# First expert's weights fetched and half split during the routing, first chunk peeled, rotary tables moved to the last chunk, in a two-layer mixture-of-experts trunk

## Chip, cores and metric

One core of one Trainium2 chip. The metric is the device time of one execution in microseconds (us), the median of several executions of the same program.

## What is computed

A two-layer trunk over 4096 tokens of width 1024, all in float32 outside. Layer 0 is a causal pooling mixer, layer 1 a sliding-window attention with rotary queries and keys; each is followed by the same hierarchical mixture of experts and a gated per-layer embedding. The change touches the mixture of experts and the place of the rotary tables:

```python
expert_id = gsel * EXPERTS_PER_GROUP + eidx         # 32 experts, 2 for each token
order = jnp.argsort(flat_e)                         # tokens sorted by expert
xs = xt[stok]
a = jax.nn.silu(lax.ragged_dot(xs, w_gate, sizes)) * lax.ragged_dot(xs, w_up, sizes)
y = lax.ragged_dot(a, w_down, sizes) * sg[:, None]
out = jnp.zeros((T, D), y.dtype).at[stok].add(y)
cos, sin = rope_tables(positions)                   # used only in and after layer 0's combining
```

Each expert has three float32 matrices (gate and up 1024x512, down 512x1024), 6 MB in all.

## The kernel before

The kernel is written as phases; each is a block with one program for each engine, and a block begins when all engines have ended the one before. In order: constants, pooling mixer, then `route_phase`, `experts_phase`, `combine_phase` for layer 0, the attention, `route_phase`, `experts_phase` for layer 1, and the final combining.

**Routing.** VectorE (DVE) works alone through a chain of some 150 small operations: group and expert of each token, a rank of each token in its expert, a table of chunks, and at last eight blocks of one-hot matrices that TensorE (PE) turns into the list of tokens. In layer 0 alone the block carries other work beside it: the embedding product `up`, 32 tiles of 24 bf16 matmuls. ScalarE (ACT) copies each half tile from PSUM to one of three buffers `up_out` (`take_up`, L568), and SyncE (SP) stores each tile (L550). PE has two PSUM banks for it, so it may be two half tiles ahead of ACT; ACT takes tile t only when the store of tile t-3 has landed. SP's program in this block is: two loads of `wu_raw`, four 1 MB loads of `pT`, then the 32 stores.

**Experts.** The sorted tokens are cut into chunks of up to three tiles of 128 rows of one expert; here there are 32 chunks in each layer, numbered q, with weights in buffer u = q mod 2. The products run in a split of float32 into two bf16 parts: for each weight chunk c of six (0, 1 gate; 2, 3 up; 4, 5 down), SP loads 1 MB into `raw[c]` (L832), ACT makes the high part `w_hi` (L883), and POOL (c = 0 to 2) or DVE (c = 3 to 5) makes the low part `w_lo` (L825). `raw` is single: the load of the next expert's c waits for the low part. The token rows are gathered by three indirect DMAs of POOL (L916) and turned by three DMA transposes of SP (L838) into the single `xT`. PE then makes gate and up for four blocks f of 128 columns, with two PSUM banks each; ACT does the silu (L894), DVE three operations for each f (`gated`, L951 to L955), and PE the down product, 24 matmuls for each tile; DVE copies it to `y` (L967), SP stores it (L857).

Steady order on SP for chunk q: loads of expert q+2, then the transposes of q+1 once gate and up of q are done, then the stores of q. On ACT for chunk q: high parts 4, 5 of q+1, four silus, high parts 0 to 3 of q+2.

**Opening of the phase.** SP loads expert 0 (in layer 0 after the rotary positions), waits for all three gathers, turns, loads expert 1 as the low parts free `raw`, and in layer 0 waits for the rotary sines and stores the tables. ACT makes six high parts, in layer 0 the two sines, then four high parts of expert 1, and only then enters the chunks and its first silu. In layer 0 DVE starts with the 11 chained rotary operations (L1124 to L1137).

## Time and profile before

| | |
|---|---|
| median of 3 runs | 5163.12 us (5152.84 to 5165.77) |
| the profiled execution | 5158.74 us |
| its span | 5157.1 us |
| PE busy | 4617.6 us (90%) |
| DVE, ACT, POOL busy | 2868.5, 1985.6, 1582.1 us |
| mean DMA rate | 232 GB/s |

The span runs from the first instruction to the last. Times in the trace count from the span's start. The routing of layer 0 stands at about 291 to 400, its experts at 400 to 1592; the routing of layer 1 at 3385 to 3472, its experts at 3472 to 4690. A busy share of an engine is an average over the stages; what a stage is worth has to be read at the wait that ends last there.

### The profile page before, as it was taken

How to read it: one execution, taken by the hardware profiler on the slowest of the kernel's cores; microseconds unless marked ns; L12 is line 12 of the kernel's file. 1: busy time of each engine (PE TensorE's matmuls, PEld its weight loads, DVE VectorE, ACT ScalarE, POOL GpSimd, SP SyncE). 2: the span in 40 equal slices, each digit the busy share in tenths (PEclk: the TensorE clock that was granted, in tenths of full speed). 3: DMA queues.
4: the chain of work that ended last, by engine and by line, in shares of the span. 5: the costliest groups of instructions: out<-in, count | busy, mean ns of one | idle time of the engine just before them, and what ended most of it. 6: DMA issues, size and time to landing. Idle time of an engine off the chain costs nothing. (4 is left out here: it accounts for less than half of the span.)

```text
span 5157.1 us, 89595 instructions
## 1 busy us (share of the span) xinstructions
PE 4617.6 (90%) x28834; PEld 2934.8 (57%) x29253; DVE 2868.5 (56%) x5893; ACT 1985.6 (39%) x2898; POOL 1582.1 (31%) x1161
## 2 busy tenths in 40 slices
PE   7985999999995999999499999936999999996999
PEld 6953766666672444444256666625666676663444
DVE  6774444444444555555388888873444444444665
ACT  6844344343432122222155555514433434332333
POOL 1104444443440111110033343304434434331332
PEclk9997999999997999999799999968999999998999
DMA  8969999999986666665377777619999999976997
GB/s 248 324 216 301 304 318 294 296 306 299 280 269 190 172 172 172 171 171 147 97 164 180 181 179 181 165 45 313 298 308 302 293 302 289 296 240 184 219 226 154
DMA packets 1265957, 1194.89 MB, mean 232 GB/s; under 512 B 945616, under 2 KB 965072, under 8 KB 1265872
## 3 DMA queue, kind: packets, MB, share of 16 engines
q1 hardware_dynamic: 1219792, 1026.04, 69.0%
q0 software_dynamic: 46080, 167.79, 10.7%
q8 instruction: 44, 0.72, 0.1%
q14 instruction: 41, 0.34, 0.0%
HBM read 717.60 MB, written 249.56 MB: 188 GB/s over the span
## 5 line engine op out<-in xcount | busy, mean ns | idle before, releaser
L825 POOL TENSOR_TENSOR ex_w_lo<-ex_raw,ex_w_hi 128x2048 bf16<-128x2048 f32 x192 | 780.7, 4094 | 1166.5 <-ACT ex_w_hi L883 1166.5
L883 ACT ACTIVATE ex_w_hi<-ex_raw 128x2048 bf16<-128x2048 f32 x384 | 707.3, 1900 | 458.8 <-PE ex_ps_y L110 189.1
L987 PE MATMUL ex_ps_gate<-ex_xT,ex_w_hi 128*128 128x0 bf16 x2048 | 571.9, 280 | 171.7 <-DMA ex_xT<-ex_xrow 130.1
L988 PE MATMUL ex_ps_gate<-ex_xT,ex_w_hi 128*128 128x0 bf16 x2048 | 571.8, 279 | 0.0
L989 PE MATMUL ex_ps_gate<-ex_xT,ex_w_lo 128*128 128x0 bf16 x2048 | 571.6, 279 | 0.0
L987 PE MATMUL ex_ps_up<-ex_xT,ex_w_hi 128*128 128x0 bf16 x2048 | 559.4, 273 | 0.0
L988 PE MATMUL ex_ps_up<-ex_xT,ex_w_hi 128*128 128x0 bf16 x2048 | 558.9, 273 | 0.0
L989 PE MATMUL ex_ps_up<-ex_xT,ex_w_lo 128*128 128x0 bf16 x2048 | 558.8, 273 | 0.0
L951 DVE TENSOR_TENSOR ex_aT<-ex_silu,ex_ps_up 128x384 bf16<-128x384 f32 x256 | 141.7, 553 | 725.5 <-PE ex_ps_up L989 549.7
L967 DVE COPY ex_y<-ex_ps_y 128x512 f32 x324 | 224.1, 692 | 567.0 <-PE ex_ps_y L110 505.3
L109 PE MATMUL ex_ps_y<-ex_w_lo,ex_aT 128*128 128x512 bf16 x1296 | 492.2, 380 | 8.5
L110 PE MATMUL ex_ps_y<-ex_w_hi,ex_aT 128*128 128x512 bf16 x1296 | 492.2, 380 | 0.0
L894 ACT ACTIVATE ex_silu<-ex_ps_gate 128x384 f32<-128x384 f32 x256 | 125.0, 490 | 900.7 <-PE ex_ps_gate L989 900.3
L825 DVE TENSOR_TENSOR ex_w_lo<-ex_raw,ex_w_hi 128x2048 bf16<-128x2048 f32 x192 | 443.6, 2312 | 19.3 <-ACT ex_w_hi L883 19.3
L1897 POOL TENSOR_TENSOR att_pr<-att_ex,att_rden 128x512 bf16<-128x512 f32 x256 | 294.4, 1150 | 518.8 <-DVE att_rden L1990 515.2
L108 PE MATMUL ex_ps_y<-ex_w_hi,ex_aT 128*128 128x512 bf16 x1134 | 431.5, 380 | 6.7 <-DVE ex_aT L955 6.7
L1920 ACT ACTIVATE att_ex<-att_score,att_nmx 128x257 f32<-128x257 f32 x512 | 256.3, 502 | 328.1 <-DVE att_nmx L1985 327.9
L987 PEld LDWEIGHTS ex_ps_gate<-ex_xT,ex_w_hi 128*128 128x128 bf16 x2048 | 204.9, 100 | 206.1 <-issue 142.8
L2077 PE MATMUL att_ps_s<-att_kT,att_qT 128*128 128x256 f32 x1024 | 270.7, 393 | 6.5 <-DVE att_kT L2040 3.1
L1980 DVE CUSTOM_DVE_ANT_0 att_score<-att_ps_s,all_mask,att_sink 128x256 f32<-128x256 f32 x496 | 218.4, 477 | 74.5 <-PE att_ps_s L2077 73.2
L108 PE MATMUL cb_ps_b<-cb_wg,cb_xT 128*128 128x512 bf16 x511 | 195.6, 383 | 59.2 <-DMA cb_xT<-cb_x 43.1
L108 PE MATMUL cb_ps_gate<-cb_wg,cb_xT 128*128 128x512 bf16 x498 | 190.7, 383 | 41.4 <-DMA cb_xT<-cb_x 41.4
(352 smaller groups left out, 9447.0 us busy)
## 6 DMA issues: line engine op xcount, KB each, us to landing
ex_raw<-in_w_exp_gate SPq DMA_DIRECT2D x128, 1024.0 KB, 10.0
ex_raw<-in_w_exp_up SPq DMA_DIRECT2D x128, 1024.0 KB, 12.8
ex_raw<-in_w_exp_down SPq DMA_DIRECT2D x128, 1024.0 KB, 6.9
y_rows<-ex_y SPq DMA_DIRECT2D x162, 512.0 KB, 2.9
cb_hin<-h_mid SPq DMA_DIRECT2D x64, 512.0 KB, 3.7
mix_x<-in_x SPq DMA_DIRECT2D x32, 512.0 KB, 4.9
h_mid<-mix_h SPq DMA_DIRECT2D x32, 512.0 KB, 5.5
y_rows<-mix_zeros SPq DMA_DIRECT2D x32, 512.0 KB, 6.1
```

What stands on the lines that cost most here:

```text
L108: pe.matmul(out, lhs_hi, rhs_hi, start=first, stop=False)
L109: pe.matmul(out, lhs_hi, rhs_lo, start=False, stop=False)
L110: return pe.matmul(out, lhs_lo, rhs_hi, start=False, stop=last)
L825: eng.tensor_tensor(w_lo[u][:, w], raw[:, c, :], w_hi[u][:, w], ALU.subtract).then_inc(lo_done, 1)
L883: act.activation(w_hi[u][:, c * WCHUNK:(c + 1) * WCHUNK], raw[:, c, :], ACT.Copy).then_inc(hi_done, 1)
L967: dve.tensor_copy(y[:, bass.ds(j, 1), 512 * n:512 * n + 512].rearrange("p o d -> p (o d)"), ps_y[n][:]).then_inc(y_done, 1)
L987: pe.matmul(out, hi, x_hi, start=j == 0, stop=False)
L988: pe.matmul(out, hi, x_lo, start=False, stop=False)
L989: mm = pe.matmul(out, lo, x_hi, start=False, stop=j == KD - 1)
L1897: pool.tensor_tensor(pr[c % ER][:, 0, :, :], ex[c % ER][:, :, 0:W], rden[:, 2 * c:2 * c + 2].unsqueeze(2).to_broadcast([P, 2, W]), ALU.mul ...
L1920: e = act.activation(ex[c % ER][:, k, :], score[c][:, k, :], ACT.Exp, bias=nmx[:, n:n + 1], accum_out=esum[:, n:n + 1])
L2077: mm = pe.matmul(ps_s[:, c % 2, :, b * P:(b + 1) * P], qT[par][:, c, :], keys[:, jj, :, :], start=True, stop=True)
```

## The change

Three things, as one edit. First, a class `ExpertWeights` owns `raw` and the first `w_hi`, so that they live through routing and experts. `route_phase` loads expert 0 (SP, six loads, behind the `pT` loads and, in layer 0, the positions; ahead of the stores of `up`), and ACT makes its six high parts there, one after every third tile of `take_up`. Second, in `experts_phase` chunk 0 is taken out of the loop. DVE makes the low parts 0 to 3 of expert 0 and POOL 4 and 5. SP turns each gathered tile as it lands, then loads expert 1 in the order 3, 0, 4, 1, 5, 2. ACT makes the high parts of expert 1 between the silus of chunk 0; DVE makes its low part 3 after `gated` 2, and 4 and 5 after the copies of chunk 0's `y`. SP turns the rows of chunk 1 ahead of the loads of expert 2. Third, the rotary angles run on DVE in the last chunk of layer 0, in three parts after f = 0, 1, 2, in the free `raw`; ACT's sines and SP's stores come after the last chunk.

```diff
@@ route_phase
+            if rot:
+                rot.load(nc, sp, A)
+            for c in range(NCHUNK):
+                W.load(sp, c, 0).then_inc(raw_loaded[c], 16)
             for t in range(tiles):
                 sp.wait_ge(up_done, 2 * t + 2)
                 sp.dma_start(up_t[t], up_out[t % UP][:]).then_inc(up_st[t % UP], 16)
@@
-            take_up(6, NT)
+            for c in range(NCHUNK):
+                take_up(6 + 3 * c, 9 + 3 * c)
+                w_hi(c)
+            take_up(6 + 3 * NCHUNK, NT)
@@ experts_phase
+            chunk(0, 0, True, True)
             with eng.Fori(0, full) as i:
-                for u in (0, 1):
-                    chunk(2 * i + u, u, True, True)
-            chunk(2 * full, 0, True, False)
-            chunk(2 * full + 1, 1, False, False)
+                chunk(2 * i + 1, 1, True, True)
+                chunk(2 * i + 2, 0, True, True)
+            chunk(2 * full + 1, 1, True, True)
+            chunk(2 * full + 2, 0, True, False)
+            chunk(2 * full + 3, 1, False, False)
@@ SP
                 for t in range(CT):
+                    if opening:
+                        sp.wait_ge(gathered[t], 16)
                     sp.dma_start(xT[:, :, :, t * P:(t + 1) * P]..., xrow[t][:], transpose=True)
@@
-            if rot:
-                rot.load(nc, sp, A)
-            e = table(sp, 2, 0, 0, NE - 1)
-            for c in range(NCHUNK):
-                load(0, c, e)
-            sp.wait_ge(gathered, 16 * CT)
-            turn_x()
             e = table(sp, 2, 1, 0, NE - 1)
-            for c in range(NCHUNK):
+            turn_x(opening=True)
+            for c in (3, 0, 4, 1, 5, 2):
                 wait_split(sp, 0, c)
-                load(1, c, e)
-            if rot:
-                rot.store(sp)
+                load(c, e)
             full = chunks(sp, chunk)
@@
             sp.sem_inc(all_stored, 1)
+            if rot:
+                rot.store(sp)
+                sp.wait_ge(rot.stored, 32)
@@ ACT
                     act.activation(silu[f % 2][:], ps_gate[f % 2][:, 0:CW], ACT.Silu).then_inc(silu_done, 1)
+                    if opening and f > 0:
+                        for c in (2 * f - 2, 2 * f - 1):
+                            hi_part(1, 1, c)
@@
-            for c in range(NCHUNK):
-                hi_part(0, 0, c)
+            chunks(act, chunk)
             if rot:
                 rot.sines(act)
-            for c in range(4):
-                hi_part(1, 1, c)
-            chunks(act, chunk)
@@ DVE
                     gated(q, f)
-                    if follows and f < NCHUNK - POOL_CHUNKS:
+                    if follows and not opening and f < NCHUNK - POOL_CHUNKS:
                         lo_part(dve, q + 1, 1 - u, POOL_CHUNKS + f, dve_lo)
+                    if opening and f == 2:
+                        lo_part(dve, 1, 1, POOL_CHUNKS, dve_lo)
+                    if rot and not follows and f == 0:
+                        rot.angles(dve)
+                    if rot and not follows and f == 1:
+                        rot.reduced(dve)
+                    if rot and not follows and f == 2:
+                        rot.bounded(dve)
```

## Rows read from the trace of the kernel before

**Rows 1.** The page's costliest groups: busy, mean ns of one, idle before and its releaser

```profile
L825 POOL TENSOR_TENSOR ex_w_lo<-ex_raw,ex_w_hi 128x2048 bf16<-128x2048 f32 x192 | 780.7, 4094 | 1166.5 <-ACT ex_w_hi L883 1166.5
...
L825 DVE TENSOR_TENSOR ex_w_lo<-ex_raw,ex_w_hi 128x2048 bf16<-128x2048 f32 x192 | 443.6, 2312 | 19.3 <-ACT ex_w_hi L883 19.3
```

**Rows 2.** Busy time by stretch, 400 to 500 us: engines, granted clock, DMA share, GB/s

```profile
400.00:500.00 100.00, 47.80 (x360) 36.89 (x365) 51.36 (x77) 42.52 (x29) 48.00 (x21) 0.73 0.98 318
```

**Rows 3.** Waits, opening of layer 0's experts (398 to 520): total, times, longest

```profile
PE ex_ps_gate L987 <- DMA ex_xT<-ex_xrow: 39.4, 2, 36.8
...
PE ex_ps_gate L987 <- ACT ex_silu L894: 16.0, 1, 16.0
```

**Rows 4.** Waits, opening of layer 1's experts (3385 to 3560)

```profile
PE ex_ps_gate L987 <- DMA ex_xT<-ex_xrow: 33.7, 1, 33.7
```

**Rows 5.** PE's waits over layer 0's steady chunks (530 to 1580)

```profile
PE ex_ps_gate L987 <- DMA ex_xT<-ex_xrow: 27.8, 12, 4.8
```

**Rows 6.** Timeline of SP's queue in layer 0's routing: start, length, instruction

```profile
292.81 7.79 SPq L546 DMA_DIRECT2D rt_pT<-pT_rows  x4
307.03 90.61 SPq L550 DMA_DIRECT2D up_rows<-rt_up_out  x32
```

**Rows 7.** DMA issues, 290 to 400: KB each, median us from issue to landing

```profile
up_rows<-rt_up_out SPq DMA_DIRECT2D x32, 512.0 KB, 2.6
rt_pT<-pT_rows SPq DMA_DIRECT2D x4, 1024.0 KB, 11.6
```

**Rows 8.** The same view, 400 to 470

```profile
rot_sin<-ex_y SPq DMA_DIRECT2D x1, 512.0 KB, 16.9
```

**Rows 9.** Timeline of ACT in layer 0's routing: idle before and releaser in brackets

```profile
313.30 0.60 ACT L568 ACTIVATE rt_up_out<-rt_ps_up 128x512 f32<-128x512 f32 x1 [0.70 <-PE rt_ps_up L110]
...
396.68 0.60 ACT L568 ACTIVATE rt_up_out<-rt_ps_up 128x512 f32<-128x512 f32 x1 [0.70 <-PE rt_ps_up L110]
```

**Rows 10.** Timeline of SP's queue, first 85 us of layer 0's experts

```profile
402.41 2.01 SPq L832 DMA_DIRECT2D ex_raw<-in_w_exp_gate  x2
...
415.00 16.07 SPq L838 DMA_TRANSPOSE ex_xT<-ex_xrow  x3
432.58 0.95 SPq L832 DMA_DIRECT2D ex_raw<-in_w_exp_gate  x2
...
475.10 7.77 SPq L838 DMA_TRANSPOSE ex_xT<-ex_xrow  x3
```

**Rows 11.** Timeline of ACT, the same stretch

```profile
426.53 1.91 ACT L883 ACTIVATE ex_w_hi<-ex_raw 128x2048 bf16<-128x2048 f32 x1 [0.80 <-DMA ex_raw<-in_w_exp_down]
...
438.57 1.91 ACT L883 ACTIVATE ex_w_hi<-ex_raw 128x2048 bf16<-128x2048 f32 x1 [6.81 <-DMA ex_raw<-in_w_exp_gate]
...
451.59 1.91 ACT L883 ACTIVATE ex_w_hi<-ex_raw 128x2048 bf16<-128x2048 f32 x1 [0.80 <-DMA ex_raw<-in_w_exp_up]
...
469.93 0.49 ACT L894 ACTIVATE ex_silu<-ex_ps_gate 128x384 f32<-128x384 f32 x1 [4.35 <-PE ex_ps_gate L989]
...
482.91 3.71 ACT L883 ACTIVATE ex_w_hi<-ex_raw 128x2048 bf16<-128x2048 f32 x2 [3.15 <-PE ex_ps_y L110]
```

**Rows 12.** Timeline of ACT, opening of layer 1's experts

```profile
3541.44 0.49 ACT L894 ACTIVATE ex_silu<-ex_ps_gate 128x384 f32<-128x384 f32 x1 [4.97 <-PE ex_ps_gate L989]
...
3559.73 3.71 ACT L883 ACTIVATE ex_w_hi<-ex_raw 128x2048 bf16<-128x2048 f32 x2 [8.22 <-PE ex_ps_y L110]
```

**Rows 13.** Timeline of POOL: the first gather of each layer's experts

```profile
403.00 1.18 POOL L916 DMA_INDIRECT ex_xrow<-hn_rows,ex_token  x1 [0.98 <-POOL ex_token L912]
...
3474.31 1.04 POOL L916 DMA_INDIRECT ex_xrow<-hn_rows,ex_token  x1 [0.87 <-POOL ex_token L912]
```

**Rows 14.** Timeline of DVE, opening of layer 0's experts

```profile
408.17 3.74 DVE L1132 SCALAR_TENSOR_TENSOR ex_y<-ex_y 128x1024 f32<-128x1024 f32 x3
...
423.20 10.10 DVE L825 TENSOR_TENSOR ex_w_lo<-ex_raw,ex_w_hi 128x2048 bf16<-128x2048 f32 x3 [0.37 <-ACT ex_w_hi L883]
```

**Rows 15.** Timeline of DVE, last chunk of layer 0's experts

```profile
1568.15 0.56 DVE L951 TENSOR_TENSOR ex_aT<-ex_silu,ex_ps_up 128x384 bf16<-128x384 f32 x1 [2.67 <-PE ex_ps_up L989]
```

More of the change, by code:

```diff
@@ L472, in _, with __init__, load, split_hi @@
             steps(pe, step)
-def route_phase(nc, A, C, layer):
+class ExpertWeights:
+    def __init__(self, nc, A, layer, stack):
+        m = Mem(nc, f"ew{layer}", stack)
+        self.mem = m
+        self.raw = m.sb("raw", [P, NCHUNK, WCHUNK])
+        self.hi = [m.sb("hi0", [P, NCHUNK * WCHUNK], BF16)]
+        self.lo = []
+        self.layer = layer
+        halves = "l e (h k p) n -> (l e h) p k n"
+        self.src = [A[n].rearrange(halves, p=P, k=WCHUNK // w)
+                    for n, w in (("w_exp_gate", F), ("w_exp_up", F), ("w_exp_down", D))]
+    def load(self, sp, c, e):
+        part, half = divmod(c, 2)
+        return sp.dma_start(self.raw[:, c, :].rearrange("p (k n) -> p k n", k=WCHUNK // (D if part == 2 else F)),
+                            self.src[part][self.layer * 2 * NE + 2 * e + half])
+    def split_hi(self, act, u, c):
+        return act.activation(self.hi[u][:, c * WCHUNK:(c + 1) * WCHUNK], self.raw[:, c, :], ACT.Copy)
+    def split_lo(self, eng, u, c):
+        w = slice(c * WCHUNK, (c + 1) * WCHUNK)
+        return eng.tensor_tensor(self.lo[u][:, w], self.raw[:, c, :], self.hi[u][:, w], ALU.subtract)
+def moe_phase(nc, A, C, layer, rot=None):
+    with ExitStack() as stack:
+        W = ExpertWeights(nc, A, layer, stack)
+        if rot:
+            rot.open(W.mem, W.raw)
+        route_phase(nc, A, C, W, layer, rot)
+        experts_phase(nc, A, C, W, layer, rot)
+def route_phase(nc, A, C, W, layer, rot=None):
     with ExitStack() as stack:
@@ L538, in route_phase @@
             "dve_step exp_in exp_out ranked summed hot_done token_done listed chunk_mm")
+        raw_loaded = [m.sem(f"raw_loaded{c}") for c in range(NCHUNK)]
         block = stack.enter_context(nc.Block())
@@ L827, in _, with load, turn_x @@
         @block.sync
         def _(sp):
-            def load(q, c, e):
-                part, half = divmod(c, 2)
-                ap = src[part][layer * 2 * NE + 2 * e + half]
-                sp.dma_start(raw[:, c, :].rearrange("p (k n) -> p k n", k=WCHUNK // (D if part == 2 else F)),
-                             ap).then_inc(raw_loaded[c], 16)
-            def turn_x():
+            def load(c, e):
+                W.load(sp, c, e).then_inc(raw_loaded[c], 16)
+            def turn_x(opening=False):
@@ L845, in chunk @@
                         wait_split(sp, q + 1, c)
-                        load(q + 2, c, e)
+                        load(c, e)
+                opening = isinstance(q, int)
+                if refill and not opening:
+                    weights()
                 first = table(sp, 0, q, 0, MAX_TILES)
@@ L854, in chunk @@
                     turn_x()
+                if opening:
+                    weights()
                 with sp.Fori(0, tiles) as j:
@@ L879, in _ @@
             act.sem_inc(down_mm, DOWN_OPEN)
+            act.sem_inc(hi_done, NCHUNK)
             def hi_part(q, u, c):
-                act.wait_ge(raw_loaded[c], 16 * q + 16)
-                act.activation(w_hi[u][:, c * WCHUNK:(c + 1) * WCHUNK], raw[:, c, :], ACT.Copy).then_inc(hi_done, 1)
+                act.wait_ge(raw_loaded[c], 16 * q)
+                W.split_hi(act, u, c).then_inc(hi_done, 1)
             def chunk(q, u, follows, refill):
-                if follows:
+                opening = isinstance(q, int)
+                if follows and not opening:
                     first = table(act, 0, q, 0, MAX_TILES)
@@ L926, in _ @@
             gather(0)
[L927 to L928 removed]
+            for c in range(DVE_FIRST, NCHUNK):
+                W.split_lo(pool, 0, c).then_inc(pool_first_lo, 1)
             pool.wait_ge(xT_turned, 16 * CT)
@@ L968, in chunk @@
                                         ps_y[n][:]).then_inc(y_done, 1)
-            for c in range(POOL_CHUNKS, NCHUNK):
-                lo_part(dve, 0, 0, c, dve_lo)
-            if rot:
-                dve.wait_ge(rot.stored, 32)
+                if opening:
+                    for c in range(POOL_CHUNKS + 1, NCHUNK):
+                        lo_part(dve, 1, 1, c, dve_lo)
+            for c in range(DVE_FIRST):
+                W.split_lo(dve, 0, c).then_inc(dve_first_lo, 1)
             chunks(dve, chunk)
@@ L1084, in open @@
         self.inv = m.sb("inv", [P, nf])
-        self.sin, self.cos, self.turns = (room[:, i, :].rearrange("p (t f) -> p t f", f=nf) for i in range(3))
+        self.sin, self.cos, self.turns = (room[:, i, 0:NT * nf].rearrange("p (t f) -> p t f", f=nf) for i in range(3))
         self.loaded, self.step_done, self.ready, self.made, self.stored = m.sems(
```

129 lines of the change are left out of this document (70 added, 59 removed).

## Prediction

> **What bounds the kernel now.** I read the shares of busy time first, then the waits of PE in three stretches, then the queues in order of time. PE is busy for 90% of the span, so the change can only win where PE stands still for long. In the steady chunks it hardly does: 27.8 us in 1050, in 12 waits for turned rows [rows 5]. At each opening it does. In layer 0 the first product waits 36.8 us for the rows (from the last `up` tile at 396.7 to 433.5), then 16.0 us more for a silu [rows 3, 9]; in layer 1 the first of these two is 33.7 us [rows 4]. In 400 to 500 PE is busy 47.8 us at a granted clock of 0.73 while DMA is at 0.98 [rows 2]. What ends last is a queue: the gathers were issued at 403.0, but the transposes stand behind 6 MB of weights, from 415.0 to 431.1, and PE starts 2.4 us after [rows 10, 13]. The second wait is ACT's order: its high parts of expert 1 (438.6 to past 451.6) come ahead of its first silu [rows 11]. The routing of layer 1 leaves DMA and ACT nearly idle; that of layer 0 does not: PE has `up` work until 396.7, and ACT and SP serve it in step, 1.30 us for each half tile [rows 9].
>
> **Loads moved into the routing.** Layer 1: six loads and six high parts (1.91 us each) lie beside 87 us of DVE work that needs ACT twice, both times ahead of them. Cost nothing.
>
> Layer 0: the six loads are issued ahead of the `up` stores on SP's queue. Is a store held by loads ahead of it? A 512 KB store lands in 2.6 us on a free queue; the rotary store issued at 440.1, behind the loads of expert 1, took 16.9 [rows 7, 8]. So it is. The last `pT` load lands near 310.5 (issued by 300.6, median 11.6 to landing) [rows 6, 7]. Then come the positions (1.5 us, my estimate for 4-byte pieces, from 0 to the 4 us they take alone), and six loads at 2.71 us each, the step between high parts that wait for landings (0.80 idle + 1.91) [rows 11]: 328.3. The first store lands at 328.3 + 1.3 (half of a load) = 329.6, say 330. ACT takes tile 3 at 313.3 [rows 9] and needs that store. It waits 17 us, and PE, two banks ahead, stops with it, before the one-hot sums that DVE's chain needs. PE restarts at the low level of its clock: 2 us more (0 to 3). The six high parts then each stand between two takes: 0.60 + 1.91 + 0.60 = 3.11 us against the 2.6 that two banks hide, so 0.5 each, 3 at most with the semaphore's delay, partly in PE's waits for DVE: 2 (0 to 8, if none of the 1.91 is hidden). PE's work ends this block, so all of it shows. **+21 us** (from 8, if the store slips in earlier than the queue's order says, to 28).
>
> The Trainium skill, "DMA: Bandwidth & Descriptors", section on queues, rings and completion order, says that on each DMA engine descriptors are consumed in ring order and SP has one row of rings. This speaks against the change: by it the store waits for all six loads, as the row of the rotary store has it; were the queue fair to later transfers, the sum would be 17 us better.
>
> **Opening of the experts.** All times are layer 0's, counted as if its block began at 400.9 as before. Gathers are issued from 403.0; with no weights in flight the first lands some 4.3 us later (estimate: 2.6 for a 512 KB transfer [rows 7] plus POOL's 1.18 and a little), 407.3. Three transposes take 7.8 us to issue in a steady chunk [rows 10], to 415.1, and PE starts 2.4 later: 417.5, 16 us sooner. Gate and up take four times 4.84 [rows 11], plus 2 for the low clock: until 438.9.
>
> Loads of expert 1 need the turn's end, and the first needs DVE's low part 3. DVE starts at about 402.7; its four parts take 9.2 us, POOL's two 8.2 [rows 1]. Side by side they would end by 412, in turns by 420. Three parts of DVE took 10.1 us where 6.9 are due, while POOL made its own [rows 14], so I take turns, 418. By landings after a first issue at 402.4 and 432.6, the fourth load lands 19.0 us on and the sixth 24.1 [rows 10, 11]: 437.1 and 442.2. ACT needs the fourth (part 1) before silu 2, and the sixth (part 2) before silu 3: part 2 until 444.1, part 3 446.0, silu 446.5. On DVE low part 3 stands ahead of `gated` 3: 446.0 + 2.3 + 1.7 = 450.0. PE has done 1.9 us of its first down group by 440.8 and waits 9 us. The down product of two tiles is 48 matmuls of the size of which six take 1.30 [rows 9], 10.4 us: it ends at 450.0 + 8.4 = 458.4. Chunk 1 started at 482.9 + 2.6 = 485.5 [rows 3, 11]. Gain 27.
>
> The Trainium skill, "SBUF — State Buffer", section on two separate sides, calls the port pair that DVE shares with GpSimd an exclusive lock, taken by an instruction of DVE with two SBUF inputs against one of GpSimd that reads. The row of 10.1 us agrees; with no lock the loads would start 3 us sooner and each opening gain 3 more.
>
> What is late next: low parts 4 and 5 of expert 1 now follow the copies of chunk 0 (459.1 + 2 x 2.3 = 463.7), and the last load of expert 2 waits for them. It lands 6.0 us on (432.6 to 438.6 [rows 10, 11]), near 469.7, and its high part, to 471.6, stands ahead of the first silu of chunk 1. PE reaches that silu's bank at 458.4 + 9.7 = 468.1: 3 us given back. Gain at chunk 2: **-24 us**.
>
> Layer 1 lies 3071.3 us later [rows 13]. PE starts at 3488.8; `gated` 3 ends at 3521.3; the down product has three tiles (15.6, less 1.9): 3535.0, against 3559.7 [rows 12]. Less 3 for chunk 1: **-22 us**. The peeled loop itself, with the same work per chunk, costs nothing that a row shows.
>
> **Rotary tables.** At the start they cost DVE and SP time that PE's waits cover, so their removal is in the sum. In the last chunk a block f has 4.28 us (2.67 idle, three operations of 1.6 in all) [rows 15]. The three parts take some 3.5 us each (the middle one is 3.74 [rows 14]; the others by similar passes), 5.1 with `gated`: DVE falls behind 0.8 us in each, and `gated` 3 comes 2.3 us later. ACT's sines lie beside the down product. SP's two stores come after the last `y` has landed: 2.6 + 1.3 + issue 0.4 = 4.3 us. **+6.6 us** (4 to 11).
>
> **Sum.** Layer 0: +21 - 24 + 6.6 = +4, no gain at all; layer 1: -22. Together -18 on the profiled execution's 5158.7 (1.6 of it around the span): 5141. That execution is 4.4 below the median of the runs, from which the sum would be 5145. I give **5143**.
>
> **Rivals.**
> - *The openings win as above, but the stores are not held back.* Layer 0's routing then costs 5 or less, the whole gain is 34 to 40: 5122. For it: the DMA share in the routing's middle leaves room. Against: the 16.9 us of the rotary store. Chance 0.13.
> - *The lead is given back (slower).* If chunks are paced by the stream of weights and not by PE, a layer keeps only what the stream gains. The last load of expert 2 was issued just ahead of the turn at 475.1 [rows 10], so it landed by about 480, and now at 470: 10 us. In layer 1, where the opening was shorter by 3 and the new one longer by a down tile's 5, half of that, 5. So 15 against 28 lost: 5158.7 + 13 = 5172. It decides if PE waits for low parts or `raw` in chunks 2 to 5. For it: DMA at 0.98 [rows 2]. Against: 27.8 us of waits in 1050 [rows 5], all for turned rows. Chance 0.10.
> - *The hold is longer or deeper.* The positions' 4-byte pieces and slower loads hold the store to 337, ACT's high parts cost their full 8, the openings lose 5 more: gain 0 to 8, 5155. Chance 0.22.
>
> The forecast itself has 0.55, with a range of its own from 5130 to 5150.
>
> **Chances and range.** Measurement tells 0.3%, 15 us, from no change. Faster by more needs below about 5146: 0.13 from the first rival and two thirds or more of the forecast's, with a little of the third: 0.56. Slower by more: 0.06, from the second rival. The rest, 0.38, is within. The range takes in the first and third rival and stops short of the second: 5118 to 5164.
>
> **What would show it.** In layer 0's routing, takes of ACT with one idle of some 17 us before tile 3, the first `up` store landing near 330 and the block ending near 418. PE's first gate product 16 us after the block's start instead of 33, no wait on silu before the down product, but one on `gated` 3. The last of the high parts of expert 2 ahead of the first silu of chunk 1. Low waits from chunk 2 on. The prediction is wrong if the take of tile 3 doesn't wait, if gathers land later than 5 us, or if PE's waits in chunks 2 to 31 exceed the 28 us of before by more than a few.

## The result: 0.3% slower, where 0.3% faster was forecast

| | before | after |
|---|---|---|
| median | 5158.52 us (17 runs, 5144.49 to 5167.69) | 5177.14 us (17 runs, 5164.42 to 5189.57) |
| ratio | | 1.0032, 95% interval 1.0023 to 1.0042 |
| span of the profiled execution | 5157.1 us | 5166.4 us |

The forecast was 5143 us with a range to 5164. The two profiled executions stand 9.3 us apart, and the ratio says 16.5. Some of the difference is in the last stage (layer 1's combining), which no edit touches: it took 466 us in the execution of before, 462 in that of after, and 460 to 474 over the ten experiments below. A single execution is good for the length of one stretch, and not for a sum to within 5 us. One execution of the seventh experiment's kernel took 10926 us at a granted clock of 0.44 and is not in its ratio.

The ledger by stages, from the first instruction of each block and the first product of each chunk (us; "opening" is from the block's start to chunk 2):

| | before | after | change | forecast |
|---|---|---|---|---|
| start of the routing, layer 0 | 291.9 | 294.5 | +2.6 | 0 |
| routing, layer 0 | 109.0 | 129.5 | +20.5 | +21 |
| opening, layer 0 | 123.2 | 113.2 | -10.0 | -24 |
| chunks 2 to 30 | 1035.2 | 1033.8 | -1.4 | 0 |
| last chunk to the next block | 32.8 | 41.1 | +8.3 | +6.6 |
| from there to layer 1's experts | 1880.6 | 1881.0 | +0.4 | 0 |
| opening, layer 1 | 120.4 | 116.2 | -4.3 | -22 |
| the rest | 1563.9 | 1557.2 | -6.7 | 0 |

Two forecast losses came as forecast; the two gains came to 14.3 instead of 46.

**Layer 0's routing.** The timeline of SP's queue, after:

```profile
303.23 2.92 SPq L1162 DMA_DIRECT2D ew_pos_i<-in_positions  x1
306.19 8.02 SPq L493 DMA_DIRECT2D ew_raw<-in_w_exp_gate  x2
...
319.89 22.47 SPq L596 DMA_DIRECT2D up_rows<-rt_up_out  x6
```

and that of ACT (the brackets give the idle time before and what ended it):

```profile
313.22 0.60 ACT L618 ACTIVATE rt_up_out<-rt_ps_up 128x512 f32<-128x512 f32 x1 [0.70 <-PE rt_ps_up L111]
333.81 1.09 ACT L618 ACTIVATE rt_up_out<-rt_ps_up 128x512 f32<-128x512 f32 x2 [19.99 <-DMA up_rows<-rt_up_out]
```

Where ACT went from one take to the next with 0.70 us of idle [rows 9], it now waits 19.99 us for a store of `up_rows`, once. The positions and the loads keep SP's queue busy issuing until 319.9, so the first store is issued there at the earliest, and it lands behind them. The positions, 16 KB in 4-byte pieces, hold the DMA engines as well. Busy time by stretch, its last two numbers the DMA share and GB/s:

```profile
311.00:314.00 3.00, 3.00 (x16) 1.37 (x14) 3.00 (x38) 1.62 (x4) 0.00 (x0) 1.00 0.70 13
```

The engines are busy for 0.70 of these 3 us and move 13 GB/s, after the last `pT` load and ahead of the first of the six.

**Layer 0's opening.** The timeline of POOL, after:

```profile
425.87 2.90 POOL L976 DMA_INDIRECT ex_xrow<-hn_rows,ex_token  x1 [0.98 <-POOL ex_token L972]
429.08 1.66 POOL L976 DMA_INDIRECT ex_xrow<-hn_rows,ex_token  x1 [0.30 <-issue]
431.05 1.90 POOL L976 DMA_INDIRECT ex_xrow<-hn_rows,ex_token  x1 [0.30 <-issue]
...
457.10 4.07 POOL L503 TENSOR_TENSOR ex_w_lo<-ew_raw,ex_w_hi 128x2048 bf16<-128x2048 f32 x1 [7.56 <-ACT ex_w_hi L498]
...
483.61 14.20 POOL L503 TENSOR_TENSOR ex_w_lo<-ew_raw,ew_hi 128x2048 bf16<-128x2048 f32 x3 [10.99 <-ACT ew_hi L498]
```

The timeline of SP's queue:

```profile
432.30 9.81 SPq L893 DMA_TRANSPOSE ex_xT<-ex_xrow  x3
442.36 0.66 SPq L493 DMA_DIRECT2D ew_raw<-in_w_exp_up  x1
...
493.90 6.45 SPq L493 DMA_DIRECT2D ew_raw<-in_w_exp_down  x2
```

Of DVE:

```profile
425.46 8.87 DVE L503 TENSOR_TENSOR ex_w_lo<-ew_raw,ew_hi 128x2048 bf16<-128x2048 f32 x4
...
457.23 0.56 DVE L1008 TENSOR_TENSOR ex_aT<-ex_silu,ex_ps_up 128x384 bf16<-128x384 f32 x1 [3.23 <-PE ex_ps_up L1058]
...
458.28 3.30 DVE L1012 TENSOR_TENSOR ex_aT<-ex_a,ex_aT 128x384 bf16<-128x384 f32 x1
...
470.31 4.46 DVE L503 TENSOR_TENSOR ex_w_lo<-ew_raw,ex_w_hi 128x2048 bf16<-128x2048 f32 x1 [2.46 <-ACT ex_w_hi L498]
...
488.02 11.94 DVE L503 TENSOR_TENSOR ex_w_lo<-ew_raw,ex_w_hi 128x2048 bf16<-128x2048 f32 x2
```

Of ACT:

```profile
470.19 0.47 ACT L953 ACTIVATE ex_silu<-ex_ps_gate 128x384 f32<-128x384 f32 x1
...
498.68 1.91 ACT L498 ACTIVATE ew_hi<-ew_raw 128x2048 bf16<-128x2048 f32 x1 [7.14 <-DMA ew_raw<-in_w_exp_down]
506.05 1.91 ACT L498 ACTIVATE ew_hi<-ew_raw 128x2048 bf16<-128x2048 f32 x1 [5.45 <-DMA ew_raw<-in_w_exp_down]
507.86 0.85 ACT L953 ACTIVATE ex_silu<-ex_ps_gate 128x384 f32<-128x384 f32 x2
```

Read them from the top. The gathers are issued at 425.87, but beside DVE's four low parts the three issues take 2.90, 1.66 and 1.90 us, where the first took 1.18 before [rows 13]. The transposes start at 432.30 and need 9.81, and PE starts at 444.41: 20.4 us after the block's start, not 16.6. The loads of expert 1 follow at 442.36, when the turn is over (442.1); DVE's four low parts were done at 434.3. Silu 3 comes at 470.19. Up to chunk 1's first product the opening is 63.1 us long, against 84.6 before: 21.4 gained.

Then half of it is lost again. At 488.02 DVE comes to low parts 4 and 5 of expert 1, 4.4 us after POOL began its three of expert 2 (483.61). DVE takes 11.94 us for two parts that are worth 4.6 by the mean of [rows 1], POOL 14.20 for three worth 12.3. The last two loads of expert 2 wait for those parts (6.45 us of issue, from 493.90 on), ACT waits for these loads, 7.14 us and 5.45 us, and its first silus stand behind: 507.86. The waits of PE, 419 to 560, total, times and longest:

```profile
PE ex_ps_gate L1056 <- DMA ex_xT<-ex_xrow: 24.9, 1, 24.9
PE ex_ps_gate L1056 <- ACT ex_silu L953: 9.6, 1, 9.6
PE ex_ps_y L109 <- DVE ex_aT L1012: 7.6, 1, 7.6
```

The same for layer 1 (3488 to 3620):

```profile
PE ex_ps_gate L1056 <- DMA ex_xT<-ex_xrow: 31.7, 2, 24.4
PE ex_ps_gate L1056 <- ACT ex_silu L953: 8.5, 1, 8.5
```

A wait costs more than its length. Granted clock (after the five engines' busy times) from the end of the 7.6 us wait to chunk 1:

```profile
476.30:487.10 10.80, 10.67 (x39) 4.37 (x41) 2.08 (x3) 3.97 (x3) 3.49 (x1) 0.78 0.96 336
```

PE is busy throughout, but at a mean of 0.78: having stood still it starts again at the lower of its two levels (1.2 GHz) and is back at 2.4 only within the stretch. The down product takes 10.8 us where 8.4 were forecast.

The 36.8 and 33.7 us of [rows 3, 4] have shrunk to 24.9 and 24.4. The wait on silu, 16.0 in [rows 3], is there with 9.6, but a chunk later. And it costs clock. Busy time by stretch (PE, PEld, DVE, ACT, POOL, granted clock, DMA share, GB/s), chunk 1 of layer 0 and of layer 1, after:

```profile
487.00:537.00 50.00, 40.39 (x266) 26.41 (x265) 28.83 (x23) 16.64 (x12) 27.99 (x10) 0.90 0.85 276
...
3561.00:3609.00 48.00, 32.27 (x244) 24.46 (x242) 24.93 (x22) 18.55 (x13) 25.29 (x9) 0.84 0.87 281
```

In chunk 1 of before the granted clock was 1.00 in both layers; it is 0.90 and 0.84 here. Chunk 1 took 50.1 us instead of 38.7, and in layer 1 47.7 instead of 33.6: 11.4 and 14.0 lost, of which 9.6 and 8.5 are the wait on silu. In layer 1 some 3.4 more are at its end: PE waits 7.4 us for turned rows ahead of chunk 2 (the second of the two waits in the 31.7 above), where it waited 4.0 for a low part of POOL before.

**Steady chunks.** PE's waits, 560 to 1560:

```profile
PE ex_ps_gate L1056 <- DMA ex_xT<-ex_xrow: 30.4, 13, 5.3
```

All for turned rows. Before the change the same stretch has 24.5 us for turned rows, 3.9 for one low part of POOL and 0.2 for `aT`: 28.6 against 30.4, the same size.

**The last chunk.** SP's queue at the end of layer 0's experts, after:

```profile
1606.67 0.34 SPq L1172 DMA_DIRECT2D rot_sin<-ew_raw  x1
...
1612.05 0.40 SPq L1298 DMA_DIRECT2D cb_g_ple<-in_g_ple  x1
```

The two stores of the tables are issued when the last `y` has landed, and the next block's first load 5.4 us after the first of them. The last chunk took 41.1 us in this execution; of the six experiments below that leave this end alone, five have 39.4 to 39.5 and one 40.9, against 32.8 before.

### The profile page after: what moved, and what is told of

Read it like the earlier page. It is cut to its first block and busy times, and to the rows that moved or that the text cites. A ratio compares the mean times of both kernels' runs of the same rounds, so it can differ in the third digit from the quotient of the medians.

```text
span 5166.4 us, 89976 instructions
## 1 busy us (share of the span) xinstructions
PE 4650.4 (90%) x29188; PEld 2937.1 (57%) x29253; DVE 2889.0 (56%) x5895; ACT 1905.0 (37%) x2839; POOL 1586.4 (31%) x1159
## 3 DMA queue, kind: packets, MB, share of 16 engines
q0 software_dynamic: 46080, 167.79, 10.6%
## 5 line engine op out<-in xcount | busy, mean ns | idle before, releaser
L503 POOL TENSOR_TENSOR ex_w_lo<-ew_raw,ex_w_hi 128x2048 bf16<-128x2048 f32 x96 | 388.6, 4074 | 591.6 <-ACT ex_w_hi L498 591.6
L503 POOL TENSOR_TENSOR ex_w_lo<-ew_raw,ew_hi 128x2048 bf16<-128x2048 f32 x94 | 387.2, 4148 | 557.8 <-ACT ew_hi L498 557.7
L498 ACT ACTIVATE ew_hi<-ew_raw 128x2048 bf16<-128x2048 f32 x192 | 353.9, 1900 | 274.0 <-PE ex_ps_y L111 166.1
L498 ACT ACTIVATE ex_w_hi<-ew_raw 128x2048 bf16<-128x2048 f32 x192 | 353.2, 1899 | 261.4 <-PE ex_ps_y L111 179.6
L1056 PE MATMUL ex_ps_gate<-ex_xT,ew_hi 128*128 128x0 bf16 x1024 | 286.3, 280 | 91.9 <-DMA ex_xT<-ex_xrow 91.9
L1056 PE MATMUL ex_ps_gate<-ex_xT,ex_w_hi 128*128 128x0 bf16 x1024 | 285.7, 279 | 47.6 <-DMA ex_xT<-ex_xrow 25.6
L1057 PE MATMUL ex_ps_gate<-ex_xT,ew_hi 128*128 128x0 bf16 x1024 | 286.4, 280 | 0.0
L1057 PE MATMUL ex_ps_gate<-ex_xT,ex_w_hi 128*128 128x0 bf16 x1024 | 285.6, 279 | 0.0
L1056 PE MATMUL ex_ps_up<-ex_xT,ex_w_hi 128*128 128x0 bf16 x1024 | 280.5, 274 | 0.0
L1057 PE MATMUL ex_ps_up<-ex_xT,ex_w_hi 128*128 128x0 bf16 x1024 | 280.4, 274 | 0.0
L1056 PE MATMUL ex_ps_up<-ex_xT,ew_hi 128*128 128x0 bf16 x1024 | 278.3, 272 | 0.0
L1057 PE MATMUL ex_ps_up<-ex_xT,ew_hi 128*128 128x0 bf16 x1024 | 278.3, 272 | 0.0
L109 PE MATMUL ex_ps_y<-ew_hi,ex_aT 128*128 128x512 bf16 x640 | 245.1, 383 | 19.1 <-DVE ex_aT L1012 19.1
## 6 DMA issues: line engine op xcount, KB each, us to landing
ew_raw<-in_w_exp_up SPq DMA_DIRECT2D x128, 1024.0 KB, 13.9
```

Of the source, the lines that this page charges most:

```text
L109: pe.matmul(out, lhs_hi, rhs_hi, start=first, stop=False)
L498: return act.activation(self.hi[u][:, c * WCHUNK:(c + 1) * WCHUNK], self.raw[:, c, :], ACT.Copy)
L503: return eng.tensor_tensor(self.lo[u][:, w], self.raw[:, c, :], self.hi[u][:, w], ALU.subtract)
L1056: pe.matmul(out, hi, x_hi, start=j == 0, stop=False)
L1057: pe.matmul(out, hi, x_lo, start=False, stop=False)
```

## Experiments

All ratios are against the kernel before, run beside them on the same chip (three chips in all, with medians of the kernel before of 5156.11, 5157.33 and 5156.26 us); the change as it stands has 1.0032. Ten kernels ran.

### Loads behind the stores they delayed

```diff
+            for c in range(0 if tiles else NCHUNK):
-            if rot:
-                rot.load(nc, sp, A)
-            for c in range(NCHUNK):
                 W.load(sp, c, 0).then_inc(raw_loaded[c], 16)
             for t in range(tiles):
                 sp.wait_ge(up_done, 2 * t + 2)
                 sp.dma_start(up_t[t], up_out[t % UP][:]).then_inc(up_st[t % UP], 16)
+                if t % 3 == 2 and t // 3 < NCHUNK:
+                    W.load(sp, t // 3, 0).then_inc(raw_loaded[t // 3], 16)
+                if rot and t == 22:
+                    rot.load(nc, sp, A)
```

> The changed kernel, but in layer 0's routing each load of expert 0 is issued right behind the store of tile 2, 5, 8, ... and no longer ahead of all stores. Ring order theory (the first store is held by the loads ahead of it on SP's queue): the 20 us pause of ACT before tile 3 goes, the routing's length falls from 125.6 us to 106 to 109 (105.3 before the change), and the whole time by some 17 to 20 us against the changed kernel, to about that of the kernel before. Rival (the 6 MB or ACT's six high parts cost the time wherever they stand): the pause is spread over the tiles and the routing stays above 118 us.

Measured: 5151.29 us (12 runs), ratio 0.9986 (0.9978 to 0.9995). The same 6 MB, the same six high parts, and the routing is 109.1 us long, as before the change. (The expectation counts the block to ACT's last take of `up`: its 105.3 and 125.6 us are the ledger's 109.0 and 129.5.) SP's queue, and ACT past the place of the pause:

```profile
307.82 5.51 SPq L594 DMA_DIRECT2D up_rows<-rt_up_out  x3
313.37 0.43 SPq L493 DMA_DIRECT2D ew_raw<-in_w_exp_gate  x1
315.59 5.51 SPq L594 DMA_DIRECT2D up_rows<-rt_up_out  x3
```

```profile
313.67 0.60 ACT L620 ACTIVATE rt_up_out<-rt_ps_up 128x512 f32<-128x512 f32 x1 [0.70 <-PE rt_ps_up L111]
```

A load now stands between stores and ACT's idle is 0.70 us as ever. So the hold was the price of where the loads stood, and the six high parts between takes, for which I had 2 us, cost nothing. The edit moves the positions too, behind store 22, and spreads the loads; this run alone doesn't say which of it counts.

### The loads on another queue

```diff
+            for c in range(NCHUNK):                       # POOL, behind the low parts of wu
+                W.load(pool, c, 0).then_inc(raw_loaded[c], 16)
-            for c in range(NCHUNK):                       # SP, ahead of the stores
-                W.load(sp, c, 0).then_inc(raw_loaded[c], 16)
```

(the positions are loaded behind store 22, as above)

> The changed kernel, but in layer 0's and 1's routing the six loads are issued at the same early time by POOL on its own queue, so they share the DMA engines with the stores but stand ahead of none of them. Ring order theory: no pause of 20 us before tile 3 (at most some 3 us from sharing), routing 106 to 111 us. Rival (the DMA engines' throughput holds the stores, whatever the queue): the pause stays at 15 us or more.

Measured: 5163.86 us (11 runs), 1.0014 (1.0005 to 1.0022); the routing is 123.1 us long (119.2 as the expectation counts). Neither side of the expectation holds wholly; the rival's 15 us is the nearer. Timeline of SP's queue, of ACT, and the landings of SP's four `pT` loads:

```profile
307.39 35.70 SPq L592 DMA_DIRECT2D up_rows<-rt_up_out  x8
```

```profile
325.87 1.08 ACT L618 ACTIVATE rt_up_out<-rt_ps_up 128x512 f32<-128x512 f32 x2 [13.33 <-DMA up_rows<-rt_up_out]
```

```profile
DMA to landing us min/median/max: 7.8/12.2/24.4
```

No load stands ahead of the first store on its queue, which is issued at 307.39, and still ACT waits 13.33 us for it. The last `pT` load took 24.4 us to land (323.14), where the one before the change landed at 310.55, and the store's landing follows 2.65 us behind it, since six more megabytes go through the same 16 DMA engines: by then four of the six loads had landed, and the last did at 331.2. So 13 of the 20 us stay when nothing of the 6 MB stands ahead of the store on its queue. The 7 that go are not the queue's order alone, for the positions no longer stand ahead of the store either; by the 3 us at 13 GB/s above, my estimate is some 3 for them and 3 to 4 for the order, and no run separates the two. The first experiment cures all of it because it also spreads the loads. The Trainium skill, "DMA: Bandwidth & Descriptors", section on queues, rings and completion order, which spoke for a wait behind everything in the same ring, can stand for no more than these 3 to 4; it is no promise that another ring is free of the rest.

### Low parts 4 and 5 ahead of POOL's

```diff
                 first = table(dve, 0, q, 0, MAX_TILES)   # DVE: behind this, the copies of y
+                if opening:                              # placed ahead of it
+                    for c in range(POOL_CHUNKS + 1, NCHUNK):
+                        lo_part(dve, 1, 1, c, dve_lo)
...
-                if opening:                              # no longer behind the copies
-                    for c in range(POOL_CHUNKS + 1, NCHUNK):
-                        lo_part(dve, 1, 1, c, dve_lo)
```

> The changed kernel, but DVE makes low parts 4 and 5 of expert 1 right after gated 3 of chunk 0, ahead of the copies of y, when POOL has no low part to make. Theory (the late low parts 4 and 5 hold the last two loads of expert 2, whose high parts stand ahead of chunk 1's first silu): they take 4.6 us in place of 11.9 and 8.8, PE's wait in chunk 1 (9.6 and 8.5 us) goes or falls under 2, the whole time falls by 12 to 20 us. Rival (the wait in chunk 1 is set by the low parts of POOL or by the turns, not by these): the wait stays above 6 us in each layer and the time falls by less than 6.

Measured: 5146.33 us (11 runs), 0.998 (0.9971 to 0.9989). DVE, and the waits of PE from 419 to 560:

```profile
476.28 4.49 DVE L503 TENSOR_TENSOR ex_w_lo<-ew_raw,ex_w_hi 128x2048 bf16<-128x2048 f32 x2
```

```profile
PE ex_ps_gate L1056 <- DMA ex_xT<-ex_xrow: 29.0, 2, 26.1
PE ex_ps_y L109 <- DVE ex_aT L1012: 7.7, 1, 7.7
```

The two parts take 4.49 us, the wait on silu is gone in both layers, chunk 1 takes 38.7 and 35.6 us at a clock of 1.00 and 0.98, and chunk 2 starts 102.6 and 106.2 us after its block instead of 113.2 and 116.2. In layer 1 PE still waits 6.0 us for turned rows ahead of chunk 2. The gain, 27 us by the ratios, is more than the 12 to 20 expected; the openings account for 20.5 of it.

### POOL waits until DVE is through

```diff
                 if refill:
+                    if isinstance(q, int):               # the peeled chunk alone
+                        pool.wait_ge(dve_lo, NCHUNK - POOL_CHUNKS)
                     for c in range(POOL_CHUNKS):
                         lo_part(pool, q + 2, u, c, pool_lo)
```

> The changed kernel, with low parts 4 and 5 of expert 1 where they are, but POOL begins its low parts of expert 2 only when DVE has made these. It isolates the exclusive use of a port by the two engines. Theory: DVE's two parts fall from 11.9 and 8.8 us to 4.6, the loads 4 and 5 of expert 2 are issued 4 to 7 us sooner, and PE's wait in chunk 1 falls from 9.6 and 8.5 us to 3 to 6; POOL's parts come later, which may cost part of it at chunk 2. Rival (the parts are long for another reason): they keep their length.

Measured: 5161.02 us (10 runs), 1.0015 (1.0004 to 1.0027). DVE and POOL:

```profile
486.88 4.48 DVE L503 TENSOR_TENSOR ex_w_lo<-ew_raw,ex_w_hi 128x2048 bf16<-128x2048 f32 x2
```

```profile
491.44 12.12 POOL L503 TENSOR_TENSOR ex_w_lo<-ew_raw,ew_hi 128x2048 bf16<-128x2048 f32 x3 [19.97 <-DVE ex_w_lo L503]
```

DVE's parts begin at the same place in its program as in the change and take 4.48 us instead of 11.94; all that differs is that POOL isn't at work beside them. POOL's three take 12.12 instead of 14.20. Chunk 1 is 6.0 us shorter in layer 0 and 3.6 in layer 1; PE still waits for its first silu 2.8 and 4.4 us. That is the price that the expectation named: POOL's parts end 80.8 us after the block's start, 73.9 in the change.

### The silus ahead of the high parts

```diff
-                if follows and not opening:              # ACT, ahead of the four silus
-                    first = table(act, 0, q, 0, MAX_TILES)
-                    act.wait_ge(down_mm, first * 2 + DOWN_OPEN)
-                    for c in (4, 5):
-                        hi_part(q + 1, 1 - u, c)
                 for f in range(KF):
+                    if follows and not opening and f == 2:
+                        first = table(act, 0, q, 0, MAX_TILES)
+                        act.wait_ge(down_mm, first * 2 + DOWN_OPEN)
+                        for c in (4, 5):
+                            hi_part(q + 1, 1 - u, c)
```

> The changed kernel, but in every chunk after the opening ACT makes the silus of f = 0 and 1 ahead of the high parts 4 and 5 of the next expert, and those of f = 2 and 3 behind them. If the wait in chunk 1 is ACT's order alone: PE's 9.6 and 8.5 us there go, and the time falls by 12 to 20 us against the changed kernel though DVE's two late low parts stay 11.9 and 8.8 us long. Rival (these parts hold the chain of weights, and so only the place of the wait moves): the wait shows at the down product of chunk 1 or at chunk 2, and the time falls by less than 8 us. In the steady chunks the order may cost or win a few us.

Measured: 5176.78 us (7 runs), 1.0036 (1.0023 to 1.0049). The waits of PE, 419 to 560:

```profile
PE ex_ps_gate L1056 <- DMA ex_xT<-ex_xrow: 34.0, 2, 25.1
PE ex_ps_y L109 <- DVE ex_aT L1012: 9.3, 2, 7.7
```

The wait on silu is gone and nothing is won: chunk 1 takes 49.4 us, and the wait stands in front of the down product (1.6 us) and of chunk 2 (8.9), whose turn, behind the late loads on SP's queue, takes 15.4 us to issue. So the order on ACT passed the delay on and did not make it; the low parts and the loads behind them are the cause.

### DVE lets the gathers go first

```diff
+            pool.sem_inc(gather_out, 1)                  # behind gather(0)
...
+            dve.wait_ge(gather_out, 1)                   # ahead of its four low parts
```

> The changed kernel, but DVE begins its first four low parts only when POOL has issued the three gathers of chunk 0. If these low parts slow the gathers' issue (2.9, 1.7 and 1.9 us each in the changed kernel against 1.2, 0.9 and 1.8 before): they fall to about 1.2, 0.9 and 0.9, the turns start 2 to 3 us sooner, and PE's first product with them, unless the low parts, now beside POOL's, hold it. Rival (the issue is slow for another reason, as the first of the phase): no change of the issue times. Whole time within 5 us of the changed kernel.

Measured: 5171.6 us (7 runs), 1.0031 (1.0019 to 1.0043). POOL:

```profile
425.80 1.18 POOL L976 DMA_INDIRECT ex_xrow<-hn_rows,ex_token  x1 [0.98 <-POOL ex_token L972]
427.28 2.39 POOL L976 DMA_INDIRECT ex_xrow<-hn_rows,ex_token  x1 [0.30 <-issue]
```

A miss: the semaphore's increment got past the gathers on POOL, DVE began at 426.56, and only the first issue was free of it. That one took 1.18 us instead of 2.90, the next, now beside DVE, 2.39 instead of 1.66. In layer 0 PE started 22.5 us after the block's start, no sooner. In layer 1, with issues of 1.04, 2.53 and 1.90 us instead of 3.01, 1.79 and 1.90, the turn began 6.2 us after the block's start instead of 7.8, PE started at 18.7 instead of 21.4, and chunk 2 at 113.1 instead of 116.2: there the expected 2 to 3 us came.

### The rotary tables back in the opening

```diff
+            if rot:                                      # DVE, behind its four low parts
+                rot.angles(dve)
+                rot.reduced(dve)
+                rot.bounded(dve)
             chunks(dve, chunk)
```

(and their calls in the last chunk taken out; the sines ahead of ACT's chunks, the stores behind the loads of expert 1, `y` as their room)

> The changed kernel without its third part: the rotary angles run on DVE in the opening behind the first low parts, the sines on ACT ahead of the first silu, the stores behind the loads of expert 1, in the buffer y. The last chunk of layer 0 with the block's end falls from 41.1 us to 33 to 34 (32.8 before the change). In the opening they lie under the gathers, the turns and the first products: if that cover holds, chunk 2 starts no later and the whole time falls by 7 to 9 us. If it does not (DVE's 12 us or the two sines come past the first gated part, or the stores hold the turns of chunk 1), the opening loses 3 to 8 us and the whole time stays.

Measured: 5164.42 us (12 runs), 1.0013 (1.0004 to 1.0022). From the last chunk's first product to the next block 32.8 us, as before the change. The opening took 114.0 us against 113.2. The third part of the change cost 8.3 us by these two traces (6.6 or 6.7 by the end of the five others) and bought 0.8 us at most.

### The three mended parts together

The first, third and seventh experiment in one kernel.

> The loads behind the stores (as in e1), low parts 4 and 5 early (as in e3), and the rotary part as before the change (as in e7), together. By the sum of the single effects, 20 + 20 + 7 us against the changed kernel, so about 5130 us where the kernel before has 5156: ratio 0.994 to 0.996. If the effects overlap (the openings' gains are given back later), it is not faster than the better of e1 and e3, 0.998.

Measured: 5125.46 us (6 runs, 5120.38 to 5131.43) beside 5157.33, ratio 0.9939 (0.9927 to 0.9952): faster than both kernels. The effects of the single traces add up: from 1.0032 x 5157.3 = 5173.8 take 20 (routing), 10.6 and 9.9 (openings) and 8.3 (end), 5125. The three ratios taken singly promise more, 24, 27 and 10 us, together some 60; the combined kernel has 48. Each of these is good to some 6 us, so the trace's sum is no proof that nothing overlaps. Waits of PE, 398 to 540:

```profile
PE ex_ps_gate L1059 <- DMA ex_xT<-ex_xrow: 25.7, 1, 25.7
...
PE ex_ps_gate L1059 <- ACT ex_silu L956: 0.9, 1, 0.9
```

In layer 1 the wait on silu is gone altogether. The routing takes 110.0 us, the openings 102.8 and 108.2, the end 32.8.

### Low parts held back until the rows are gathered, and until they are turned

Both on top of the three mended parts. In the first DVE alone waits, for the third gather's landing; in the second DVE and POOL wait for the transposes:

```diff
+            dve.wait_ge(gathered[CT - 1], 16)            # first kernel
...
+            dve.wait_ge(xT_turned, 16 * CT)              # second kernel
             for c in range(DVE_FIRST):
                 W.split_lo(dve, 0, c).then_inc(dve_first_lo, 1)
...
+            pool.wait_ge(xT_turned, 16 * CT)             # second kernel, ahead of POOL's two
```

> The three mended parts, and DVE holds back its first low parts until the third gather has landed. Open is why PE starts 20 to 22 us after the experts' block in the opening, where 16.6 was forecast: the gathers' issues took 6.5 us in all where 3.9 were due, and the three transposes 9.8 to 11.7 us where a steady chunk has 7.8. Theory A (both engines' memory ports: DVE's two-input low parts slow the gathers' issues, and the late third gather stretches the transposes): the three issues take about 1.2, 0.95 and 0.95 us, the transposes are issued from about 7 us after the block's start and take 8, PE starts 17 to 18 us after it; DVE's parts then end near 21 us after it, and the time is 5122 to 5124 us beside a kernel before at 5157 (ratio 0.993), since PE now waits a little for low parts. Theory B (the transposes are slow by themselves in the opening, cold or first of their kind): the gathers are short, but the transposes take 10 us or more and PE starts 20 us or more after the block. The time is then as the three mended parts alone, 0.994.

> The three mended parts, and DVE and GpSimd both hold back their first low parts until the turns are done, so that nothing at all runs on them beside gathers and transposes. Theory A: issues 1.2, 0.95, 0.95 us, transposes in 7.8 to 8 us; the turned rows are there 16 to 17 us after the block's start. Theory B: transposes 10 us or more all the same. PE then waits for the low parts (2.3 us for the first one) and the loads of expert 1 are issued some 5 us later, so the time is no better than that of the three mended parts: 0.994 to 0.996.

Measured: 5133.2 us (5 runs), 0.9956 (0.9943 to 0.997), and 5153.39 us (10 runs), 0.9993 (0.9983 to 1.0004), neither better than the three mended parts alone (0.9939, 0.9927 to 0.9952): the second is slower, the first probably so, though the two intervals overlap. The first was expected at 0.993. POOL, SP and DVE of the first kernel:

```profile
403.86 1.18 POOL L979 DMA_INDIRECT ex_xrow<-hn_rows,ex_token  x1 [0.98 <-POOL ex_token L975]
...
406.59 0.94 POOL L979 DMA_INDIRECT ex_xrow<-hn_rows,ex_token  x1 [0.30 <-issue]
```

```profile
408.49 8.85 SPq L897 DMA_TRANSPOSE ex_xT<-ex_xrow  x3
424.62 0.42 SPq L493 DMA_DIRECT2D ew_raw<-in_w_exp_up  x1
```

```profile
412.62 11.78 DVE L503 TENSOR_TENSOR ex_w_lo<-ew_raw,ew_hi 128x2048 bf16<-128x2048 f32 x4 [9.07 <-DMA ex_xrow<-hn_rows,ex_token]
```

With DVE quiet the issues take 1.18, 0.94 and 0.94 us, and the transposes begin 6.6 us after the block's start (401.94) instead of 8.1 to 8.4. Their issue takes 8.85 us, and 8.90 in the second kernel, where POOL is quiet too: much of the 9.8 to 13.9 us of the other kernels was the late third gather, for whose rows the third transposition waits. Even here these landed at 412.62 (DVE's release), 4.1 us into the turn. That is theory A. The 7.8 us of a steady chunk, by which I judged, is one chunk's: over layer 0's chunks from 2 on the same kernel has a median of 8.1 and up to 11.8, so 8.9 is nothing that the opening has to explain. PE starts at 420.24, 18.3 us after the block, by then held by DVE's low part. The gain is spent at once: DVE's parts come late and so do the loads (424.62), 22.7 us after the block where the three mended parts alone had 19.2. In layer 0 the tables' operations follow on DVE, ahead of the first `aT`, and the opening takes 109.3 us against 102.8; in layer 1, without them, 105.6 against 108.2. The tables out of the way in layer 0 as well might make a kernel a little better than the three mended parts; that wasn't run. DVE and POOL of the second kernel, both starting at the turn's end:

```profile
425.27 16.62 DVE L503 TENSOR_TENSOR ex_w_lo<-ew_raw,ew_hi 128x2048 bf16<-128x2048 f32 x4 [15.87 <-DMA ex_xT<-ex_xrow]
```

```profile
425.32 12.22 POOL L503 TENSOR_TENSOR ex_w_lo<-ew_raw,ew_hi 128x2048 bf16<-128x2048 f32 x2 [11.95 <-DMA ex_xT<-ex_xrow]
```

Started together, four parts of DVE took 16.62 us and POOL's two 12.22. Alone they are worth 9.2 and 8.2; the two together 17.4. They took turns: taken singly, each of POOL's two and of DVE's second and third is recorded at 6.10 to 6.15 us, which is its own time and nearly all of the neighbour's, while DVE's first and last took 2.29 and 2.28. The expectation missed what this costs: it had PE wait 2.3 us behind the turn for the first low part, but PE needs both of gate's, and the second stands behind one of POOL's (2.3 + 4.1 + 2.3). PE started 26.1 and 26.0 us after the block's start, 8.6 behind the turn in layer 0, and the openings took 120.7 and 119.2.

## Why the forecast was wrong

**The step that failed is the opening of the experts, -24 and -22; they gave -10.0 and -4.3.** It failed in two terms.

- *"Low parts 4 and 5 ... 463.7 ... 3 us given back."* I saw which work would be late next and put DVE's two parts at their mean of 2.3 us each, though I had priced the same collision for the first low parts just before. I did not ask what POOL does at that time. They took 11.9 and 8.8 us, and chunk 1 lost 11.4 and 14.0 us in place of 3. Shown from both sides: move DVE's parts, and the loss is gone (-27 us by the ratio, -20.5 by the openings in the trace); hold POOL back at the same place, and they take 4.48. The `gated` operations say the same: beside one low part of POOL (457.10 to 461.2), the one with an input in PSUM took 0.56 us and the one with both inputs in SBUF 3.30. Rearranging ACT changes nothing. This term is 19 of the 32 us that the openings missed.
- *"Part 2 until 444.1 ... gated 3 ... 450.0 + 8.4 = 458.4."* Chunk 1 should have started 57.5 us after the block and started 63.1 us after it (layer 1: 62.3 forecast, 68.5 measured). In layer 0 the loads were issued 1.3 us late, DVE's low part 3 took 4.46 us in place of 2.3, beside a low part of POOL, and `gated` 3 ended 52.3 us after the block, not 49.1. Then the down product ran at the low clock: 2.4 more. In layer 1 the loads were 2.6 late, low part 3 again took 4.46 and the down product 1.6 more. The same collision is in it twice, as low part 3 and, by slower gathers, as a late turn. That the loads were only 1.3 us late in layer 0 is luck: I had them wait for DVE's low part 3, 17.1 us after the block's start, but DVE's four parts were done after 10.4, since POOL was at its gathers and not at its low parts, and the late turn held the loads until 18.2.
- PE's start itself, 20.4 and 21.4 us after the block in place of 16.6 and 16.1, was a miss that cost little: it shortened the wait ahead of `gated` 3 to 7.6 from 9. In the ninth experiment PE starts 3.0 and 5.8 us sooner than with the three mended parts alone, with the loads no sooner, and of that 2.6 us arrive at chunk 2 in layer 1 and none in layer 0.

The Trainium skill, "SBUF — State Buffer", section on who interferes with whom, calls the port pair of DVE and GpSimd an exclusive lock, under which the later one fully blocks; the trace agrees, with 11.94 against 4.48 us and with 16.6 us for 17.4 of work.

**The hold of the stores, +21, measured +20.5.** The size was right; the mechanism only in part. The second experiment leaves 13 of the 20 us in place with no load ahead of the store on its queue: these come from sharing the DMA engines. The queue's order and the positions divide the other 7. My sum of six loads at 2.71 us each covered the sharing as well, since it counted the time to move 6 MB through. The pause was 20.0 us and not 17: the first `up` store landed 39.3 us after the block's start and not 38.1 (the positions took about 3 us and not 1.5), ACT was due for tile 3 some 1.3 sooner in its block than before the change, and 0.7 is its usual idle. Against that the high parts, 2 in the sum, cost nothing. That the total is off by 0.5 only is in part luck.

**The rotary end, +6.6, measured +8.3,** within its 4 to 11; the other kernels with the same end have 6.6 to 8.1, five of six at most 6.7.

**Routing of layer 1, 0:** 87.5 us before, 87.7 after. **Peeling by itself, 0:** chunks 2 to 30 took 1035.2 and 1033.8 us, 1031.6 to 1037.6 in all kernels. The prediction calls the steady waits "all for turned rows"; the view of [rows 5] has beside them this line, which changes no term:

```profile
PE ex_ps_gate L987 <- POOL ex_w_lo L825: 3.9, 1, 3.9
```

**The rivals.** *The lead is given back* foresaw the sign and nearly the number (5172), in part by another way: it had the chunks paced by the stream of weights in chunks 2 to 5, and of PE's waits there none is put down to a low part or to `raw`. What was given back went in chunk 1. There the weights of expert 2 did hold PE, by way of ACT's order, but because two low parts were slow, and not because DMA was full. *The hold is longer or deeper* gave 5155; of the 7 us by which it had the store later 1.2 came, its 8 for the high parts didn't, and the openings lost far more than its 5. *Stores not held back* (5122) is refuted twice: they were held, and in the first experiment, where they weren't, the time was 5151, since the openings don't give what that rival took over from my sum.

**What stays open.** How the 7 us that another queue saves divide between the positions and the queue's order. Whether the single ratios, 60 us in sum, promise more than the combined kernel's 48 by noise alone or because the effects overlap in part. And 2.6 us by which the routing started later: the eleven other executions start it between 291.9 and 297.2, so a single execution can't tell it from nothing.

## What to carry to other kernels

When an edit moves an operation of DVE with two SBUF inputs, look up what GpSimd does in the new stretch, and price both together as the sum of their times; do it for every place that the lead reaches, the one after the gain too. Prefetch through a queue that also carries stores someone waits for piece by piece between the stores, and not as a block, on whichever queue. A lead at the start of a phase is only worth what the first stretch with no slack lets through: follow the chain two chunks on before taking it as gain.

## What the runs showed of the hardware

- GpSimd's issue of a gather is slowed by DVE's two-input operations as well: 2.90, 1.66 and 1.90 us beside DVE's low parts, 1.18, 0.94 and 0.94 without.
- A small operation of DVE with both inputs in SBUF pays the rest of a neighbour's: a `gated` step of 0.56 us took 3.30 beside a GpSimd low part of 4.07 and ended 0.4 us after it. One with an input in PSUM, beside the same low part, took its 0.56.
- With 6 MB moved to another engine's DMA queue, and the positions out of the way, the first store on SP's queue still came 13 us late instead of 20.
- A load of 16 KB in 4-byte pieces kept the DMA engines busy for 0.70 of 3 us at 13 GB/s.
- PE's waits in chunk 1 (9.6 us; in layer 1 8.5 and, at its end, 7.4) also cost granted clock: 0.90 and 0.84 over the chunk, against 1.00 in both layers before.
